# Seven block products for eight in 18 of 22 slots of an FFN's first product

## What is computed

```python
x = x + rmsnorm(merged @ w_out[l], norm_mix_post[l])
h = rmsnorm(x, norm_ffn_pre[l])
gate, up = jnp.split(h @ w_ffn_in[l], 2, axis=-1)
x = x + rmsnorm((jax.nn.silu(gate) * up) @ w_ffn_out[l], norm_ffn_post[l])
```

## Time and profile before

| what | value |
|---|---|
| median of three runs | 968.33 us (966.88 to 968.61) |
| the profiled execution's own time | 966.86 us |
| its span, first to last instruction | 965.1 us |
| PE busy | 951.5 us, 99% |
| DVE, ACT, POOL busy | 521.0, 378.9, 434.8 us |
| FFN's first product, from the first slot's scaling to the last slot's | 614.4 to 837.1 us |

### The profile page before, as it was taken

How to read it: one execution, slowest core, us unless ns; L and a number is a source line. 1 busy time by engine, 2 the same in 40 slices (tenths; PEclk the granted TensorE clock), 3 DMA queues, 4 the chain that set the end, 5 groups by cost and what they waited for, 6 DMA issues and landing times.

```text
span 965.1 us, 15020 instructions
## 1 busy us (share of the span) xinstructions
PE 951.5 (99%) x6138; PEld 771.1 (80%) x6138; DVE 521.0 (54%) x718; ACT 378.9 (39%) x507; POOL 434.8 (45%) x349
## 2 busy tenths in 40 slices
PE   9999999999999999999999999999999999999996
PEld 7887877887787778777778888888888888888885
DVE  5877876856577755889667639622222232311114
ACT  6424516533551562346653426422322233222322
POOL 4874424433272253343044664444454444554550
PEclk9999999999999999999999999999999999999998
DMA  8333322332333274237164652234333342223212
GB/s 272 122 99 120 102 96 88 131 131 68 131 131 111 85 249 136 78 122 270 67 215 155 240 187 76 78 101 117 95 87 87 102 115 87 88 90 125 92 44 87
DMA packets 107767, 117.74 MB, mean 122 GB/s; under 512 B 2881, under 2 KB 86849, under 8 KB 107713
## 3 DMA queue, kind: packets, MB, share of 16 engines
q1 hardware_dynamic: 99792, 100.70, 32.6%
q10 hardware_dynamic: 7920, 16.25, 4.4%
HBM read 100.70 MB, written 16.25 MB: 121 GB/s over the span
## 4 chain that ended last, share of the span: by engine, by line
issue 37%; PE 37%; POOL 22%; DVE 2%; ACT 1%; DMA 0%; POOLq 0%; SPq 0%; DVEq 0%; ACTq 0%
POOL w_lo L591 22%; PE ps L1596 12%; PE ps L1597 12%; PE ps L1598 12%; DVE x_ct L1142 1%; DVE row L1034 1%; DVE x L1036 1%; DVE rstd_x L1065 0%; DMA w_raw<-w_in 0%; DVE proj L1072 0%; ACT w_hi L688 0%; POOL wide_mask L638 0%; ACT L694 0%; ACT squares L692 0%; POOLq L652 0%
## 5 line engine op out<-in xcount | busy, mean ns | idle before, releaser
L591 POOL TENSOR_TENSOR w_lo<-w_raw,w_hi 128x512 fp32r<-128x512 f32 x296 | 413.5, 1428 | 492.8 <-ACT w_hi L688 492.4
L688 ACT CAST w_hi<-w_raw 128x2048 fp32r<-128x2048 f32 x74 | 141.1, 1906 | 139.8 <-PE ps L1598 115.8
L1711 PE MATMUL ps<-a_hi,w_hi 128*128 128x512 f32 x384 | 155.9, 406 | 1.0 <-ACT spill_buf L774 0.9
L1596 PE MATMUL ps<-a_hi,w_hi 128*128 128x512 f32 (+1 forms) x400 | 152.8, 382 | 0.1
L1711 PE MATMUL ps<-a_lo,w_hi 128*128 128x512 f32 x384 | 152.5, 397 | 0.0
L1597 PE MATMUL ps<-a_lo,w_hi 128*128 128x512 f32 (+1 forms) x400 | 152.2, 381 | 0.0
L1598 PE MATMUL ps<-a_hi,w_lo 128*128 128x512 f32 (+1 forms) x400 | 152.2, 381 | 0.0
L1711 PE MATMUL ps<-a_hi,w_lo 128*128 128x512 f32 x384 | 151.4, 394 | 0.0
L1557 DVE TENSOR_TENSOR f_gate<-ps,g_up 128x512 f32<-128x512 f32 x22 | 15.2, 692 | 156.3 <-PE ps L1598 156.1
L1596 PEld LDWEIGHTS ps<-a_hi,w_hi 128*128 128x128 f32 x400 | 75.2, 188 | 15.3 <-POOL w_lo L591 0.7
L1711 PEld LDWEIGHTS ps<-a_hi,w_hi 128*128 128x128 f32 x384 | 72.1, 188 | 19.1 <-issue 1.7
(11 more groups left out here) (319 smaller groups left out, 1492.9 us busy)
## 6 DMA issues: line engine op xcount, KB each, us to landing
w_raw<-w_in SPq DMA_DIRECT2D x32, 1024.0 KB, 5.1
w_raw<-w_ffn_in SPq DMA_DIRECT2D x44, 512.0 KB, 4.7
spill<-spill_buf ACTq DMA_DIRECT2D x27, 512.0 KB, 3.3
w_raw<-w_ffn_out SPq DMA_DIRECT2D x11, 1024.0 KB, 4.9
w_raw<-w_branch SPq DMA_DIRECT2D x5, 1024.0 KB, 8.0
g_ab<-spill SPq DMA_DIRECT2D x8, 512.0 KB, 4.7
w_raw<-w_out SPq DMA_DIRECT2D x4, 1024.0 KB, 7.3
proj<-spill SPq DMA_DIRECT2D x1, 3072.0 KB, 14.9
```

The lines of the kernel that those rows point to most:

```text
L591: g.tensor_tensor(w_lo[:, b, c], w_raw[:, b, c], w_hi[:, b, c].bitcast(F), ALU.subtract).then_inc(lo_ready, 1)
L688: s.copy(w_hi[:, b], w_raw[:, b]).then_inc(hi_ready, 1)
L1596: t_.matmul(dst, w0, a0, start=first, stop=False)
L1711: last = t_.matmul(ps[:, 6 + half], w[:, kt, half * P:(half + 1) * P], a, start=(kt == 0 and step == 0), stop=(kt == KT - 1 and step == 2))
```

## The change

The first four slots of the product stay (`N_PLAIN = 4`). The other 18 (`N_MIX`) are computed by the Winograd form of Strassen's algorithm. The 2 x 2 blocks are: the weights' row tiles 0 to 3 and 4 to 7 by gate and up columns, and the activations' row tiles 0 to 3 and 4 to 7 by early and late tokens. Seven products of 4 row tiles x 3 passes, 84 matmuls of 256 columns, take the place of eight (48 of 512). They accumulate in PSUM where they can: `p1`, `u2`, `u3`, `c21` on one bank, `c11` on a copy of `p1`, `q5` and `c12` on a third.

The activations' seven forms (`A11, S1, A12, S2, RS, S3, A22`, each 128 x 1024 elements) are made once. For that `a_hi + a_lo` is summed by DMA (a copy of 2 MB from SP, then two accumulating DMAs of 1 MB from POOL), normalised by DVE (`norm`, four operations of 1024 elements), and mixed (`mixed_forms`, four of 1024). Each form is rounded and negated by ACT, and its low part comes from an accumulating DMA of 512 KB (`form_low`).

For every mixed slot DVE makes four sums of weight blocks of 512 elements (`t12` two, `t3`, `t4`) and one low part (`t4_low`), and six operations of 256 elements after the products (`gate_of_1`, `less_u2`, `act_1`, `up_of_2`, `act_2` two). ACT rounds blocks of 1024 (`b_high`, `t12_high`, `late_high`, and `late_high` also negates 1024) and 512 (`t4_high`), copies `p1` and `q5` out of their banks (256 each) and makes two sigmoids of 256. POOL makes two low parts of 1024 (`b_low`, `t12_low`) and issues one accumulating DMA of 512 KB (`late_low`). The weights' buffer of slot s is free when `b_low`, `t4` and that DMA are done. Buffers of `a_hi` and `a_lo` serve from then on for `late_hi`, `late_lo` and the small tiles. The load of `gain_ffn` moves from ahead of the product to behind the last `c21`, and the second product's first slot is cut in four, between the last products.

Cut to its core, the diff is:

```diff
-    S_FOUT = S_FIN + N_FIN
+    N_PLAIN = 4
+    N_MIX = N_FIN - N_PLAIN
+    S_FOUT = S_FIN + N_PLAIN
...
+        lo_groups = [[A11], [S1, A12], [S2, RS, S3], [A22]]
...
+        x_bank = lambda s: (4, 1, 5)[s % 3]
+        y_mix_bank = lambda s: 6 + s % 2
+        z_mix_bank = lambda s: 2 + s % 2
...
+                if n == 2:
+                    sp.wait_ge(h_hi_ready, 2 * NT)
+                    sp.dma_start(a_norm[:], a_hi[:].bitcast(F)).then_inc(a_copied.sem, 16)
+                load(S_FIN + n, [(dst[:, :, 0], wf2[n, 0]), (dst[:, :, 1], wf2[n, 1])])
...
+                sp.wait_ge(b_lo_made.sem, b_lo_made.base + s + 1)
+                sp.wait_ge(t4_made.sem, t4_made.base + s + 1)
+                if s == 0:
+                    sp.wait_ge(late_lo_first.sem, late_lo_first.base + 1)
+                else:
+                    sp.wait_ge(late_lo_landed[s % 2].sem, late_lo_landed[s % 2].base + 16 * ((s + 1) // 2))
...
+                    mix_raw_free(s - 2)
+                dst = w_raw[:, mix_buf(s)].rearrange("p (half k c) -> p half k c", k=KT, half=2)
+                for half in range(2):
+                    sp.dma_start(dst[:, half], wf2[N_PLAIN + s, half]).then_inc(mix_loaded[s % 2].sem, 16)
...
+            def form_low(f):
+
+                pool.wait_ge(form_neg_ready.sem, form_neg_ready.base + FORM_ORDER.index(f) + 1)
+                pool.dma_start(form_lo[f][:], form_raw(f), accum_op=ALU.add).then_inc(lo_group_landed[group_of(f)], 16)
+
+            def b_low(s):
+
+                b = mix_buf(s)
+                pool.wait_ge(b_hi_made.sem, b_hi_made.base + s + 1)
+                g.tensor_tensor(w_lo[:, b, 0:2 * BLK], w_raw[:, b, 0:2 * BLK], w_hi[:, b, 0:2 * BLK].bitcast(F),
+                                ALU.subtract).then_inc(b_lo_made.sem, 1)
+
+            def t12_low(s):
+
+                b = mix_buf(s)
+                pool.wait_ge(t12_hi_made.sem, t12_hi_made.base + s + 1)
+                g.tensor_tensor(w_lo[:, b, 2 * BLK:], t12_raw[:], w_hi[:, b, 2 * BLK:].bitcast(F),
+                                ALU.subtract).then_inc(t12_lo_made.sem, 1)
+
+            def late_low(s):
+
+                pool.wait_ge(late_neg_made.sem, late_neg_made.base + s)
+                pool.dma_start(late_lo[:, s % 2, 0:2 * BLK], w_raw[:, mix_buf(s), 2 * BLK:],
+                               accum_op=ALU.add).then_inc(late_lo_landed[s % 2].sem, 16)
+
+            low(S_FIN + 1, (S_FIN + 1) % 2)
+            pool.wait_ge(a_copied.sem, a_copied.base + 16)
+            pool.wait_ge(h_lo_ready, 2 * NT)
+            for half, k in enumerate((K1, K2)):
+                pool.dma_start(a_norm[:, k], a_lo[:, k].bitcast(F), accum_op=ALU.add).then_inc(a_summed[half].sem, 16)
+            low(S_FIN + 2, (S_FIN + 2) % 2)
+            form_low(A11)
+            low(S_FIN + 3, (S_FIN + 3) % 2)
+            form_low(S1)
+            form_low(A12)
+            b_low(0)
+            form_low(S2)
+            t12_low(0)
+            form_low(RS)
+            form_low(S3)
+            b_low(1)
+            t12_low(1)
+            late_low(1)
+            form_low(A22)
+            for n in range(N_MIX - 2):
+                b_low(n + 2)
+                t12_low(n + 2)
+                late_low(n + 2)
...
+                s.copy(form_hi[f][:], form_raw(f)).then_inc(form_hi_ready.sem, 1)
+                s.activation(form_lo[f][:], form_raw(f), ACT.Copy, scale=-1.0).then_inc(form_neg_ready.sem, 1)
...
+                act.wait_ge(mix_loaded[m % 2].sem, mix_loaded[m % 2].base + 32 * (m // 2 + 1))
+                if m < 2:
+                    act.wait_ge(slot_used, S_FOUT + m - 1)
+                else:
+                    act.wait_ge(c11_done.sem, c11_done.base + m - 1)
+                s.copy(w_hi[:, b, 0:2 * BLK], w_raw[:, b, 0:2 * BLK]).then_inc(b_hi_made.sem, 1)
...
+            def late_high(m):
+
+                b = mix_buf(m)
+                act.wait_ge(t3_made.sem, t3_made.base + m + 1)
+                if m < 2:
+                    act.wait_ge(slot_used, S_FOUT)
+                else:
+                    act.wait_ge(u3_done.sem, u3_done.base + m - 1)
+                s.copy(late_hi[:, m % 2, 0:2 * BLK], w_raw[:, b, 2 * BLK:]).then_inc(late_hi_made.sem, 1)
+                if m > 0:
+                    s.activation(late_lo[:, m % 2, 0:2 * BLK], w_raw[:, b, 2 * BLK:], ACT.Copy, scale=-1.0).then_inc(late_neg_made.sem, 1)
...
+            def sigmoid_1(m):
+
+                act.wait_ge(c11_done.sem, c11_done.base + m + 1)
+                if m > 0:
+                    act.wait_ge(f1_made.sem, f1_made.base + m)
+                s.activation(gate_1[:], c11_ps(m), ACT.Sigmoid).then_inc(sig1_ready.sem, 1)
...
+            plain_sigmoid(0)
+            plain_high(2)
+            form_high(A11)
+            plain_sigmoid(1)
+            plain_high(3)
+            form_high(S1)
+            form_high(A12)
+            plain_sigmoid(2)
+            b_high(0)
+            form_high(S2)
+            t12_high(0)
+            form_high(RS)
+            form_high(S3)
+            b_high(1)
+            plain_sigmoid(3)
+            keep_p1(0)
+            t12_high(1)
+            keep_q5(0)
+            late_high(0)
+            t4_high(0)
+            sigmoid_1(0)
+            late_high(1)
+            form_high(A22)
+            for n in range(N_MIX):
+                if n > 0:
+                    sigmoid_1(n)
+                if n + 2 < N_MIX:
+                    b_high(n + 2)
+                if n + 1 < N_MIX:
+                    keep_p1(n + 1)
+                if n + 2 < N_MIX:
+                    t12_high(n + 2)
+                else:
+                    first_out_high(n + 2 - N_MIX)
+                if n > 0:
+                    sigmoid_2(n - 1)
+                if n + 1 < N_MIX:
+                    t4_high(n + 1)
+                    keep_q5(n + 1)
+                if n + 2 < N_MIX:
+                    late_high(n + 2)
+                else:
+                    f_high(n + 2 - N_MIX)
...
+                    dve.wait_ge(a_summed[j // 2].sem, a_summed[j // 2].base + 16)
+                k = slice(2 * j, 2 * j + 2)
+                v.tensor_tensor(a_norm[:, k], a_norm[:, k], row_scale[:].unsqueeze(1).broadcast_to((P, 2, SEQ)),
+                                ALU.mult).then_inc(a_normed.sem, 1)
...
+                v.tensor_tensor(s_block[S1], late_1, late_2, ALU.subtract).then_inc(s_made.sem, 1)
+                dve.wait_ge(s_made.sem, s_made.base + 1)
+                v.tensor_tensor(s_block[S2], s_block[S1], a_block[A11], ALU.subtract).then_inc(s_made.sem, 1)
+                v.tensor_tensor(s_block[S3], a_block[A11], late_1, ALU.subtract).then_inc(s_made.sem, 1)
+                dve.wait_ge(s_made.sem, s_made.base + 2)
+                v.tensor_tensor(s_block[RS], s_block[S2], a_block[A12], ALU.add).then_inc(s_made.sem, 1)
...
+                v.tensor_tensor(t12_raw[:, 0:BLK], raw_block(s, 0), raw_block(s, 2), ALU.add).then_inc(t1_made.sem, 1)
+                dve.wait_ge(t1_made.sem, t1_made.base + s + 1)
+                v.tensor_tensor(t12_raw[:, BLK:], t12_raw[:, 0:BLK], raw_block(s, 3), ALU.add).then_inc(t2_made.sem, 1)
+
+            def t3(s):
+
+                v.tensor_tensor(raw_block(s, 2), raw_block(s, 2), raw_block(s, 3), ALU.add).then_inc(t3_made.sem, 1)
...
+            plain_act(0)
+            for j in range(4):
+                norm(j)
+            plain_act(1)
+            mixed_forms()
+            plain_act(2)
+            t12(0)
+            t3(0)
+            plain_act(3)
+            t4(0)
+            t12(1)
+            first_late_low()
+            t4_low(0)
+            t3(1)
+            t4(1)
+            for n in range(N_MIX):
+                gate_of_1(n)
+                less_u2(n)
+                if n + 2 < N_MIX:
+                    t12(n + 2)
+                    t3(n + 2)
+                if n > 0:
+                    act_2(n - 1)
+                if n + 1 < N_MIX:
+                    t4_low(n + 1)
+                if n + 2 < N_MIX:
+                    t4(n + 2)
+                act_1(n)
+                up_of_2(n)
...
+                for k in range(KT // 2):
+                    c = slice(at + k * P, at + (k + 1) * P)
+                    t_.matmul(dst, hi[:, c], form_hi[f][:, k], start=first and k == 0, stop=False, skip_group_check=not first)
+                    t_.matmul(dst, hi[:, c], form_lo[f][:, k], start=False, stop=False, skip_group_check=not first)
+                    last = t_.matmul(dst, lo[:, c], form_hi[f][:, k], start=False, stop=k == KT // 2 - 1, skip_group_check=not first)
+                return last
...
+            def c12(s):
+
+                form_ready(s, RS)
+                if s == 0:
+                    pe.wait_ge(late_lo_first.sem, late_lo_first.base + 1)
+                else:
+                    pe.wait_ge(late_lo_landed[s % 2].sem, late_lo_landed[s % 2].base + 16 * ((s + 1) // 2))
```

(100 more changed lines are left out.)

283 lines of the change are left out of this document (221 added, 62 removed).

## The result

The changed kernel takes **976.77 us** (975.31 to 978.12, 4 runs) where the kernel before takes 967.61 (966.66 to 968.61, 4 runs): 1.0097 times as long, interval 1.0084 to 1.0111. It was forecast at 963.4. The profiled execution took 975.31, its span is 973.6 against 965.1, and of the forecast's three terms (-15.6 for the matmuls, +2.7 for the ring, +8 for the start) the last has failed. The busy table and the table by stage come first; they answer to the earlier trace rows.

The account below looks back on a forecast made before the run. PE, busy 99% of the span at full clock, was taken to bound the kernel. Matmuls -15.6, ring +2.7 and start +8 sum to -4.9, from the median 968.3 to 963.4 us; range 954.5 to 976.

Parts of the forecast that it names:

- the ring: Mixed slots: DVE, ACT and POOL operations repeat at 10.2 us against PE's 10.04; 2.7 us given back over 18 slots.
- the start: Work added once, before and into the first mixed slots: PE waits of 2.5, 4 and 1.5, together 8 us.
- The pace: Mixed slots: 256-column matmuls 119.5 ns apart, 10.04 us a slot against 10.91, saving 15.6 us over 18 slots.
- Rival D: Mixed slots: alternating tiles at 130 ns make a slot 10.92, as before; 976.3 us, chance 0.05.
- rival B: Mixed slots: DVE and POOL pace PE at 10.4 to 11.3 us a slot; 972.5 us, chance 0.21.
- before u2(0): First mixed slot: PE there at 648, waiting for the forms S2, RS, S3 until 652; 4 us.
- keep_p1(0): First mixed slot: this ACT copy comes late behind sigmoid and forms; 1.5 us more of PE waiting.
- the second lands at 621: Start: the second 1 MB accumulating DMA of a_hi + a_lo lands at 621, taking one and a half times a copy.
- three of 512 KB land in 4: Start: the accumulating DMAs for the low parts of S2, RS, S3 land in 4 us, at 652.
- Rival C: Start: the accumulation is slow and the start costs 16 us; 971.4 us, chance 0.17.
- norm(2) after 627: Start: the third normalising DVE operation starting after 627 would show that the accumulation is slow.
- The cover of the steady late transfers: Mixed slots: late low parts' DMA has 9 us for issue and landing and needs under 6; nothing lost.

Follow-up runs that it names:

- the first experiment: All accumulating DMAs of the changed kernel made plain copies from the same queue, the additions left out: 972.41 us, 1.0058.

## Why the prediction was wrong

- **The pace held.** 120.0 ns for 119.5, 14.9 us saved for 15.6; the difference is that 84 x 0.120 is 10.08. Rival D falls.
- **The ring was right, its price nearly.** It turns in 10.25 us, forecast 10.2. The 2.7 us were 1.5: the term took the ring's excess over TensorE as paid in all 18 slots, where the first slots' waits give the ring a lead that lasts until 758. In 8 slots after that TensorE waits once a slot for VectorE, the sign that was named for rival B, but at the forecast's ring and not at B's 10.4 to 11.3. The ring made 0.7 us longer gave +13.7, so the point from which it decides lay, as put, within a few tenths of a microsecond.
- **The step that failed is the start: 8 us, bounds 2 and 16, measured 21.8.** Two of its three waits came with nearly the forecast's length, 2.58 us in slot four for 2.5 and 4.10 before u2(0) for 4. The second is partly luck: TensorE was there at 655.3 for 648 and the forms landed at 659.4 for 652. The third, 1.5 for keep_p1(0), did not come. What the sum had at nothing made the difference: q5(0)'s wait of 2.96 for A12's low part, c21(0)'s of 2.69 for up_2, smaller ones and the clock. One by one:
  1. "the second lands at 621" was 625.3. The factor of one and a half held (13.0 for 8.5, 4.6 for 3.0), but the plain copy under it was taken too short: those of the first experiment took 9.1 us for the 2 MB (DMA share 0.84) and a median of 8.5 for each 1 MB after it (share 1.04), where I had computed 5.5 plus 1.2 for 2 MB from the stores' mean rate.
  2. "three of 512 KB land in 4" took 7.1 to 10.2 each (issued from 643.1 to 650.4, landed by 659.4).
  3. Slot one's weights, which the sum did not touch, took 11.24 beside them, and b_high(1), waiting for them, held up the sigmoid and with it VectorE.
  4. The fill of the ring (t12, late parts, up_2 of the first two slots) had no term: c21(0) waited 2.7 us at 676.
  5. With each wait of some 3 us in this kernel TensorE's granted clock fell to its lower level, 0.21 us between short matmuls: 6.3 us in all, for which the sum had no term.
- Rival C named a part of it, the slow accumulation, with 971.4. But its sign, norm(2) after 627, did not come (625.28), and taking the add out gives back 4.4 us; the other 19 are cover, order, clock and the ring. How they divide no run shows.
- **The Trainium skill** ("Collectives: The Full Stack", section "The bandwidth ceiling: the fold count and why AG ≠ RS ≠ AR") has the adding transfers of a ReduceScatter run at half the rate of copies, because each reads two sources. By that estimate the sums land at 624; they landed at 625.3. Less the 1.2 us that I took as fixed, 4.6 and 3.0 make 3.4 and 1.8, a ratio of 1.9: in the steady slots the trace agrees. Among the other transfers of the start 13.0 and 8.5 make 1.6.
- The cover of the steady late transfers (4.6 us landed, 9 allowed), the end (no wait from 841 on) and the late gain load came out at nothing, as forecast.

## What to carry to other kernels

A change that makes an operand in another form has a start of its own; lay it out as a schedule of every queue, the loads that share the DMA engines and the orders in which an engine waits for a load ahead of something that another engine needs, before summing the steady saving. Allow for the slower clock that a wait can bring. Where engines form a ring close to the bound's pace, the ring is a wall: its share of busy time says nothing, one short instruction more is paid in every turn. A lead hides this at first, and a wait of 0.1 us a turn stands in no table of busy time; compare starts, one turn with the next. And cover may be worth more than the saving: two slots left as they were cost 1.7 us of the gain and, together with the order of the start and the fill set by following waits back to their first late step, turned +1.0% into −0.36%.
